# A four-layer hybrid encoder trunk on one core: first norm summed in x's own layout, output stored tile by tile, convolution state stored as rows

## The reference

```python
def rms_norm(x, gain):
    return x * rsqrt(mean(x * x, axis=-1) + 1e-6) * gain

for i in range(4):                                  # hp: prompt, hs: sample
    h = h + mixer_i(rms_norm(h, norm_mix[i]))
    h = h + square(relu(rms_norm(h, norm_mlp[i]) @ w_up[i])) @ w_down[i]
y = rms_norm(h, norm_final)

def short_conv_mix(h, conv_prefix, w_in, w_conv, w_out):
    gate_b, gate_c, xp = split(h @ w_in, 3)
    u_ext = concat([conv_prefix, gate_c * xp])
    y = w_conv[0] * u_ext[0:t] + w_conv[1] * u_ext[1:t+1] + w_conv[2] * u_ext[2:t+2]
    return (gate_b * y) @ w_out, u_ext[-2:]          # last 2 rows: the new state
```

## Time and profile before

| | |
|---|---|
| median of 3 runs | 2972.03 us (2965.87 to 2976.87) |
| profiled execution, its own time | 2968.8 us |
| its span | 2967.1 us |
| busy: TensorE, DVE, ScalarE, GpSimd | 96%, 43%, 29%, 9% |
| granted TensorE clock, mean | 0.982 |
| loaded, stored | 208.56 MB, 12.86 MB |
| slab of weights, issue to landing | 5.1 to 5.3 us, conv_w_out 15.4 (medians) |

### The profile page before, as it was taken

The page is one execution under the profiler, slowest core; times in us unless marked ns, Lnnn a source line. Parts: engine busy times, 40 slices in busy tenths (PEclk is TensorE's granted clock), DMA queues, the critical chain, the costliest instruction groups (busy, mean ns, idle before and its releaser), DMA issues.

```text
span 2967.1 us, 49404 instructions
## 1 busy us (share of the span) xinstructions
PE 2853.6 (96%) x21191; PEld 2767.3 (93%) x21191; DVE 1270.7 (43%) x1628; ACT 859.0 (29%) x891; POOL 258.5 (9%) x246
## 2 busy tenths in 40 slices
PE   5999999999999999999996789999999999999998
PEld 5987899999999999999996779999999878999997
DVE  3346443333455433334346554333443464433333
ACT  3126432222311322223123243212231264322222
POOL 5000100000112100001004430000010001000001
PEclk8999999999999999999998889999999999999999
DMA  3220232222223322222221012222232202322221
GB/s 122 82 74 1 72 112 77 85 85 85 84 73 71 85 86 85 77 80 85 74 70 50 1 60 83 85 85 86 72 99 85 75 1 72 117 73 84 85 85 46
DMA packets 205446, 223.39 MB, mean 75 GB/s; under 512 B 3734, under 2 KB 200416, under 8 KB 205312
## 3 DMA queue, kind: packets, MB, share of 16 engines
q1 hardware_dynamic: 200336, 203.70, 21.9%
q0 software_dynamic: 4976, 17.74, 1.8%
HBM read 208.56 MB, written 12.86 MB: 75 GB/s over the span
## 4 chain that ended last, share of the span: by engine, by line
PE 78%; issue 15%; DVE 3%; ACT 2%; POOL 1%; DMA 1%; POOLq 0%; DVEq 0%; SPq 0%; ACTq 0%
PE bank L347 67%; PE bank L453 4%; PE bank L427 2%; DMA raw<-in_conv_w_out 1%; PE bank L596 1%; POOL big L1443 1%; ACT big L802 1%; PE bank L484 1%; PE bank L420 1%; PE bank L641 0%; PE bank L650 0%; PE bank L638 0%; DVE stg L1246 0%; DVE stg L1273 0%; PE bank L547 0%
## 5 line engine op out<-in xcount | busy, mean ns | idle before, releaser
L347 PE MATMUL bank<-ahi,whi 128*128 128x288 f32 x3584 | 770.0, 296 | 7.0 <-DVE alo L1013 6.5
L347 PE MATMUL bank<-ahi,wlo 128*128 128x288 f32 x3584 | 767.2, 296 | 0.0
L347 PE MATMUL bank<-alo,whi 128*128 128x288 f32 x3584 | 766.9, 296 | 0.0
L689 ACT ACTIVATE whi<-raw 128x2048 fp32r<-128x2048 f32 x191 | 364.6, 1909 | 849.7 <-PE bank L347 838.4
L347 PEld LDWEIGHTS bank<-ahi,whi 128*128 128x128 f32 x3584 | 578.3, 189 | 9.9 <-DVE wlo L986 7.4
L347 PEld LDWEIGHTS bank<-alo,whi 128*128 128x128 f32 x3584 | 577.9, 189 | 0.0
L347 PEld LDWEIGHTS bank<-ahi,wlo 128*128 128x128 f32 x3584 | 577.7, 189 | 0.0
L347 PE MATMUL bank<-hhi,whi 128*128 128x288 f32 x2560 | 551.6, 297 | 15.6 <-DVE hlo L1163 9.5
L347 PE MATMUL bank<-hhi,wlo 128*128 128x288 f32 x2560 | 549.9, 296 | 0.0
L347 PE MATMUL bank<-hlo,whi 128*128 128x288 f32 x2560 | 549.9, 297 | 0.0
L986 DVE TENSOR_TENSOR wlo<-raw,whi 128x2048 fp32r<-128x2048 f32 x192 | 440.2, 2293 | 252.0 <-ACT whi L689 250.0
(11 more groups left out here) (252 smaller groups left out, 1769.5 us busy)
## 6 DMA issues: line engine op xcount, KB each, us to landing
raw<-in_mlp_w_up SPq DMA_DIRECT2D x64, 1024.0 KB, 5.3
raw<-in_mlp_w_down SPq DMA_DIRECT2D x64, 1024.0 KB, 5.1
raw<-in_sb_w_qkv SPq DMA_DIRECT2D x24, 1024.0 KB, 5.1
raw<-in_conv_w_in SPq DMA_DIRECT2D x12, 1024.0 KB, 5.1
raw<-in_gla_w_in SPq DMA_DIRECT2D x12, 1024.0 KB, 5.3
raw<-in_sb_w_o SPq DMA_DIRECT2D x8, 1024.0 KB, 5.2
out<-mixs POOLq DMA_DIRECT2D x3, 2048.0 KB, 7.9
out<-big POOLq DMA_DIRECT2D x2, 2048.0 KB, 8.3
```

Of the source, the lines that this page charges most:

```text
L347: mm = pe.matmul(acc[h][:, 0:HALF], w[:, u, k, m * P:(m + 1) * P], a[:, k, h * HALF:(h + 1) * HALF], start=(k == 0 and w is whi and a is a ...
L689: act.activation(whi[:, 1 - u], raw[:, 1 - u], ACT.Copy).then_inc(w_hi, 1)
```

## The change

- **First norm.** ScalarE squares each x tile as it was loaded (tokens on partitions) and sums along the row (`token_squares`, result `x_sq` [128 x 5]). GpSimd multiplies `ident` with each column of `x_sq` into `ssq` (`token_sums`), so that `sum_squares` sums over a diagonal matrix. The eight `squared` and `add_squares(0)` are gone.
- **Start of the queues.** GpSimd makes `ident` first, then issues the vector loads, then the other constants and the sums; `rank_raw` and `CK` are issued behind them. TensorE's first transposes wait for `ident_ready` alone. ScalarE splits slab 0 before it evacuates the vectors.
- **Convolution state.** `tails` is transposed on TensorE behind the first chunk of layer 1's output projection, copied to `tails_t` [32 x 128] by DVE, and stored in four DMAs of 8 rows of 512 bytes behind `add_squares(3)`.
- **Output.** Chunks 0 to 5 of `big` are transposed between chunks of the last projection (chunks 0 to 3 of all tiles, and 4 and 5 of the prompt's), chunks 0 to 3 evacuated unscaled; the rest follows after it. The last square isn't added by GpSimd but summed by TensorE apart. Five DMAs on SyncE store one token tile each.

```diff
@@ -317,6 +321,12 @@
...
+    for t in range(NT):
+        dst, n = (y_prompt[0, t * P:(t + 1) * P, :], P) if t < 4 else (y_sample[0], TS)
+        sp.wait_ge(y_v, t + 2)
+        sp.wait_ge(y_a, t + 1)
+        sp.dma_start(dst, VT[0:n, t, :]).then_inc(y_stored, 16)
+    sp.wait_ge(y_stored, 16 * NT)
@@ -360,6 +370,8 @@
...
         pe.wait_ge(ssq_add, 9 * (i + 1))
+        if i == 0:
+            pe.wait_ge(const_ready, CONSTS)
@@ -371,7 +383,7 @@
...
-    pe.wait_ge(const_ready, CONSTS)
+    pe.wait_ge(ident_ready, 1)
@@ -651,6 +663,36 @@
...
+    def y_chunk(t, c, bk):
+        w = P if t < 4 else TS
+        i = c % 4 * P
+        return pe.transpose(bk[0:w, i:i + P], big[:, c, t * P:t * P + w], ident[:])
+    def y_transposes(s, m):
+        if (s, m) == (2, 0):
+            pe.wait_ge(y_ev, 4)
+            for t in range(4):
+                for c in range(4):
+                    mm = y_chunk(t, c, bank[4 + t])
+                mm.then_inc(y_tp, 1)
+        elif (s, m) == (2, 1):
+            pe.wait_ge(y_raw, 1)
+            for c in range(4):
+                mm = y_chunk(4, c, bank[4])
+            mm.then_inc(y_tp, 1)
+        elif (s, m) == (3, 0):
+            pe.wait_ge(y_ev, 6)
+            pe.wait_ge(y_raw, 5)
+            for t in range(4):
+                for c in (4, 5):
+                    y_chunk(t, c, bank[4 + t])
+    def tails_out_(s, m):
+        if (s, m) == (0, 0):
+            pe.wait_ge(tails_ready, KC)
+            pe.transpose(bank[4][0:4 * KC, 0:P], tails[:].rearrange("p j i c -> p (j i c)"), ident[:]).then_inc(tails_tp, 1)
@@ -660,22 +702,32 @@
...
         project(base + IN_SLABS, hhi, hlo, mix_ready, 8 * layer, OUT_SLABS,
-                between=keys_out(layer // 3) if layer in (0, 3) else None)
+                between=keys_out(layer // 3) if layer in (0, 3) else tails_out_ if layer == 1 else None)
...
             project(b, ahi, alo, xg_ready, 16 * layer + 8, OUT_SLABS, norm=2 * layer + 1 if g == 0 else None)
-            project(b + OUT_SLABS, hhi, hlo, hid_ready, 8 * (GROUPS * layer + g), OUT_SLABS)
-    pe.wait_ge(acc_free, 2 * SLABS + 4)
-    pe.wait_ge(ssq_add, 9 * 9)
+            project(b + OUT_SLABS, hhi, hlo, hid_ready, 8 * (GROUPS * layer + g), OUT_SLABS,
+                    between=y_transposes if (layer, g) == (3, GROUPS - 1) else None)
+    pe.wait_ge(y_ev, 7)
     for t in range(NT):
-        w = P if t < 4 else TS
-        mm = pe.matmul(bank[0][0:w, t:t + 1], ssq[:, t * P:t * P + w], negones[:, 0:1], start=True, stop=True)
-    mm.then_inc(norm_sum, 1)
+        for c in (6,) if t < 4 else (4, 5, 6):
+            y_chunk(t, c, bank[4 + t] if t < 4 else bank[0])
+    def row_sums(src, start):
+        for t in range(NT):
+            w = P if t < 4 else TS
+            mm = pe.matmul(bank[1][0:w, t:t + 1], src[:, t * P:t * P + w], negones[:, 0:1],
+                           start=start and t == 0, stop=not start, skip_group_check=True)
+        return mm
+    pe.wait_ge(ssq_add, 9 * 8 + KC)
+    row_sums(ssq, True)
+    pe.wait_ge(sq_ready, 8 * 8 + KC)
+    row_sums(sq_x, False).then_inc(norm_sum, 1)
     pe.wait_ge(y_ev, 8)
-    pe.wait_ge(norm_v, 5 * 8 + 1)
-    to_token_major(TB_Y, big, 0)
+    for t in range(NT):
+        y_chunk(t, 7, bank[4 + t] if t < 4 else bank[0]).then_inc(y_tp, 1)
@@ -739,18 +791,26 @@
...
+    def token_squares(t):
+        n = P if t < 4 else TS
+        act.wait_ge(x_in[t], 16)
+        act.activation(stg[0:n, 0:D], flat(0, 9)[0:n, t * D:(t + 1) * D], ACT.Square,
+                       accum_out=x_sq[0:n, t:t + 1]).then_inc(x_squared, 1)
+        act.wait_ge(x_squared, t + 1)
+    act.sem_inc(sq_ready, 8)
+    for t in range(4):
+        token_squares(t)
...
         evacuate(c, X[:, c, 0:TP], bank[c][:, :])
+    token_squares(4)
+    act.wait_ge(slab_in[0], 16)
+    act.activation(whi[:, 0], raw[:, 0], ACT.Copy).then_inc(w_hi, 1)
...
     act.wait_ge(ev_a, 5)
-    act.wait_ge(slab_in[0], 16)
-    act.activation(whi[:, 0], raw[:, 0], ACT.Copy).then_inc(w_hi, 1)
...
         gained(0, j, V_MIX)
-    for j in range(KC):
-        act.wait_ge(ssq_add, j + 1)
-        squared(0, j)
@@ -922,6 +982,12 @@
...
+    def y_unscaled(s, m):
+        for t in range(4) if (s, m) == (2, 0) else (4,) if (s, m) == (2, 1) else ():
+            w = P if t < 4 else TS
+            act.wait_ge(y_tp, t + 1)
+            act.activation(VT[0:w, t, 0:512], bank[4 + t % 4][0:w, :], ACT.Copy).then_inc(y_raw, 1)
@@ -967,12 +1034,10 @@
...
     act.wait_ge(norm_v, 5 * 8 + 5)
-    for n in range((TB_Y + 1) % 2, 10, 2):
-        t, g = n // 2, n % 2
-        w = P if t < 4 else TS
-        act.wait_ge(tp_ready, TB_Y + n + 1)
-        act.activation(VT[0:w, t, g * 512:(g + 1) * 512], bank[(TB_Y + n) % 8][0:w, :], ACT.Copy,
-                       scale=rt[0:w, t:t + 1]).then_inc(ev_a, 1)
+    for t in range(NT):
+        w, bk = (P, bank[4 + t]) if t < 4 else (TS, bank[0])
+        act.wait_ge(y_tp, NT + t + 1)
+        act.activation(VT[0:w, t, 512:1024], bk[0:w, :], ACT.Copy, scale=rt[0:w, t:t + 1]).then_inc(y_a, 1)
@@ -1321,6 +1386,11 @@
...
+    def tails_rows(s, m):
+        if (s, m) == (0, 0):
+            dve.wait_ge(tails_tp, 1)
+            dve.tensor_copy(tails_t[:], bank[4][0:4 * KC, 0:P]).then_inc(tails_out, 1)
@@ -1374,26 +1444,36 @@
...
+    dve.memset(rt_m[:], 1.0).then_inc(y_v, 1)
     dve.wait_ge(norm_sum, 9)
-    dve.memset(rt_m[:], 1.0).then_inc(y_ev, 1)
-    dve.wait_ge(y_ev, 9)
-    dve.tensor_scalar(rt_m[:, 0:4], bank[0][:, 0:4], -1 / (TRI * D), EPS, ALU.mult, ALU.add)
-    dve.tensor_scalar(rt_m[0:TS, 4:5], bank[0][0:TS, 4:5], -1 / (TRI * D), EPS, ALU.mult,
+    dve.wait_ge(y_v, 1)
+    dve.tensor_scalar(rt_m[:, 0:4], bank[1][:, 0:4], -1 / (TRI * D), EPS, ALU.mult, ALU.add)
+    dve.tensor_scalar(rt_m[0:TS, 4:5], bank[1][0:TS, 4:5], -1 / (TRI * D), EPS, ALU.mult,
...
     dve.wait_ge(norm_v, 5 * 8 + 5)
-    for n in range((TB_Y + 0) % 2, 10, 2):
-        t, g = n // 2, n % 2
+    dve.wait_ge(y_raw, NT)
+    for t in range(NT):
         w = P if t < 4 else TS
-        dve.wait_ge(tp_ready, TB_Y + n + 1)
-        dve.tensor_scalar(VT[0:w, t, g * 512:(g + 1) * 512], bank[(TB_Y + n) % 8][0:w, :], rt[0:w, t:t + 1],
-                          None, ALU.mult).then_inc(ev_v, 1)
+        dve.tensor_scalar(VT[0:w, t, 0:512], VT[0:w, t, 0:512], rt[0:w, t:t + 1], None,
+                          ALU.mult).then_inc(y_v, 1)
...
+    steps = [0]
+    def made(ins):
+        ins.then_inc(pool_step, 1)
+        steps[0] += 1
+        pool.wait_ge(pool_step, steps[0])
+    made(pool.memset(ident[:], 0.0))
+    pool.affine_select(ident[:], ident[:], [[-1, P]], ALU.not_equal, 1.0, base=0,
+                       channel_multiplier=1).then_inc(ident_ready, 1)
@@ -1404,32 +1484,18 @@
...
         row += n
-    pool.dma_start(rank_raw[:], gla_w_in[0].rearrange("(k p) c -> p k c", p=P)[:, :, 3 * D:3 * D + 16])\
-        .then_inc(rank_in, 16)
-    pool.dma_start(CK, cache_sb_k[0, 0].rearrange("(j p) h d -> p j (h d)", p=P)).then_inc(ck_in, 16)
-    steps = [0]
-    def made(ins):
-        ins.then_inc(pool_step, 1)
-        steps[0] += 1
-        pool.wait_ge(pool_step, steps[0])
-    made(pool.memset(ident[:], 0.0))
-    pool.affine_select(ident[:], ident[:], [[-1, P]], ALU.not_equal, 1.0, base=0,
-                       channel_multiplier=1).then_inc(const_ready, 1)
...
     pool.tensor_copy(sums[:, 0, :], tri[:]).then_inc(const_ready, 1)
+    pool.wait_ge(const_ready, 1)
...
     pool.tensor_scalar(maskb[:], mask01[:], 1.0, -MASKED, ALU.subtract, ALU.mult).then_inc(const_ready, 1)
-    pool.wait_ge(const_ready, 5)
+    pool.wait_ge(ident_ready, 1)
@@ -1437,12 +1503,24 @@
...
         pool.memset(ssq, 0.0).then_inc(ssq_add, 1)
-        with pool.Fori(0, KC) as j:
+        with pool.Fori(0, KC if i < 8 else KC - 1) as j:
...
-    add_squares(0)
+    def token_sums():
+        made(pool.memset(ssq, 0.0))
+        for t in range(NT):
+            n = P if t < 4 else TS
+            pool.wait_ge(x_squared, t + 1)
+            pool.tensor_scalar(ssq[0:n, t * P:t * P + n], ident[0:n, 0:n], x_sq[0:n, t:t + 1], None,
+                               ALU.mult).then_inc(ssq_add, 1)
+        pool.sem_inc(ssq_add, 4)
+    token_sums()
+    pool.dma_start(rank_raw[:], gla_w_in[0].rearrange("(k p) c -> p k c", p=P)[:, :, 3 * D:3 * D + 16])                .then_inc(rank_in, 16)
+    pool.dma_start(CK, cache_sb_k[0, 0].rearrange("(j p) h d -> p j (h d)", p=P)).then_inc(ck_in, 16)
@@ -1485,17 +1563,21 @@
...
                 pool.wait_ge(y_ready, 3 * (c - 1))
+            if c >= 2:
+                pool.wait_ge(tails_ready, c - 1)
...
             pool.tensor_copy(tails[:, 0, :, c], u[:, 512:514])
-            made(pool.tensor_copy(tails[:, 1, :, c], u[:, 578:580]))
+            pool.tensor_copy(tails[:, 1, :, c], u[:, 578:580]).then_inc(tails_ready, 1)
+    def tails_stored():
+        pool.wait_ge(tails_out, 1)
...
             for j, dst in ((0, conv_p), (1, conv_s)):
```

(14 more changed lines are left out.)

11 lines of the change are left out of this document (8 added, 3 removed).

## The result

| | before | after |
|---|---|---|
| median, us | 2968.95 (4 runs, 2962.03 to 2976.87) | 2924.99 (4 runs, 2923.11 to 2927.15) |
| profiled execution, us (span) | 2968.8 (2967.1) | 2927.15 (2925.4) |
| mean granted clock | 0.982 | 0.986 |

The ratio is 0.9851, 95% interval 0.9823 to 0.9879: 44 us faster. 2938 was forecast and 2929 to 2949 given as the range, so the sign held and the size did not. The two spans differ by 41.7 us, and they are taken apart here stage by stage.

What follows compares the result with a forecast made beforehand. TensorE, busy 96% of the span, was taken as the bound. Start 20.0, middle 8.1 and end 5.1 sum to 33.2 us: 2968.8 profiled becomes 2935.6, with 3.2 to the median 2938.8; forecast 2938, range 2929 to 2949.

Steps and rivals of the forecast that it cites:

- The three places: Start, convolution output weights in the middle, and end, where TensorE stands or runs at low clock: 20.0, 8.1 and 5.1 us.
- rival (a): Start: slab 0 no earlier, or GpSimd's masks slow the first splits; gain 14.4 instead of 20.0 us, 2944; chance 0.09.
- (d): First norm: sum of squares comes late on GpSimd and TensorE still stands some 10 us; 2948; chance 0.03.
- (e): First projection: the clock stays at its lower level throughout, 153 us lost; 3092; chance 0.01.
- rival (c): Middle: the slab is late for a reason other than the stores, so 8 us stay; 2946; chance 0.03.
- the bound of 8.4: Middle: upper bound in us on the gain from replacing the element-wise convolution-state stores, forecast at net 8.1, lower bound 6.
- From issue to span's end it is 9.7 us: End: time for storing 2.36 MB, read from the kernel before and kept for five stores, as splitting costs nothing.
- Rival (b): End: the five stores don't overlap, 25 us instead of 9.7, so 15 more; 2953; chance 0.09 with its milder form.
- The estimate of 15.4 us: End: store time if the skill's fixed cost of about 2.0 us per DMA came one behind the other; 2944.
- The rule against one step: End: skill's rule that transposes don't count for the clock gate, risking 2 us on row sums; the forecast followed the trace.
- The step that failed: Whole kernel: TensorE's matmuls keep their time, so only its standing and low-clock time can be won; 33.2 us in all.
- at 6.40 us each: First projection: time per chunk of 48 matmuls, kept from before, 147.2 us for the 23 remaining chunks.

Runs made afterwards that it cites:

- old_sum: The changed kernel with the first norm sum made as before, by ScalarE squares and GpSimd additions; its first projection ends at 189.6 us, where the change's ends at 174.99.
- loads_early: The changed kernel with the loads of rank_raw and the key cache issued right behind the vector loads, as before; 2923.14 us, first matmul 3.3 us later.
- stores_late: The kernel before, its element-wise convolution-state stores issued where the change issues its row stores; 8.2 us gained, 7.4 of them lost again by the next layer.
- pool_stores: The changed kernel with its five output stores issued from GpSimd's queue instead of SyncE's; span 2922.8 us, ending 15.7 behind the last projection matmul.
- one_store: The changed kernel with the output stored by SyncE as two stores behind the last scaling, instead of five; span 2938.6 us, ending 15.7 behind the last projection matmul.
- the pair with the pace fixed: The change and the kernel before, each with three 48-column matmuls and one 192-column matmul added per projection following a norm sum; 2940.64 and 2979.74 us, both slow-paced.
- pace_probe2: The changed kernel with one unread matmul of 24, 40 or 48 columns behind the third chunk of each of the 32 MLP projections; span 2921.0 us.

## Why the prediction was right or wrong

- **Which places to read.** The three places were the right ones, and each gave what its rows said: 20.5, 8.1 and 6.7 us against 20.0, 8.1 and 5.1.
- **Start.** Slab 0 landed at 13.3 (13.5 forecast), the first matmul came at 18.51 (18.6), and the second chunk at 27.75 (28.2). old_sum splits this into 14.6 for the sum and 5.9 for the rest, and rival (a) is out. The rest is 3.3 for the loads, shown by loads_early, and, as the difference, about 2.6 for the order of the start, which wasn't tried alone. Rivals (d) and (e) did not happen.
- **Middle.** The slab landed in a median of 4.9 us, and no wait and no low clock followed. stores_late adds that the pieces and not the moment of the stores are the cause, so rival (c) is out. The size varies with the execution, from 8.1 to 12.9 us, as the jammed slab takes 32.8 to 36.8 to land; the bound of 8.4 was read from one execution and was too tight.
- **End.** 5.3 to the first store was forecast as 5.4, and 3.0 us for 28 transposes was met as well. The step that was mis-sized is "From issue to span's end it is 9.7 us": that row was a store by GpSimd, and by SyncE it is 8.2. pool_stores brings 9.9 back. Rival (b) is out: five stores took 8.2 us from the first issue to the end, and one_store's two took 8.1. The estimate of 15.4 us beside it put the stores one behind the other, which neither queue did: from GpSimd five took 9.9.
- **The rule against one step.** The row sums stand behind seven transposes, and the granted clock over them is 1.00. Twenty records take 2.20 us, where ten took 2.15 before. The chain's row and the stretch:

```profile
2912.69 2.20 PE bank L720 x20
```

```profile
2913.00:2915.00 2.00, 2.00 (x19) 1.94 (x19) 0.44 (x4) 0.56 (x1) 0.00 (x0) 1.00 0.00 0
```

 So the choice held. For the rule of the Trainium skill, "TensorE: Matmul & The Clock Gate", Part 4, it is a weak test, since here the transposes follow long matmuls closely.
- **The step that failed** is "its matmuls are untouched by this change, so what can be won is the time in which it stands or runs at the lower of its two clock levels". In the sum it is the constant of "at 6.40 us each": matmuls that the change does not touch were put at the same time as before, and a second pace at the same clock at nothing. For the first projection the constant held, 147.24 against 147.2. But untouched matmuls run at 130.0 or 133.3 ns, for up to 3072 in a row, and which of the two mostly changes by nanoseconds at the third chunk behind a norm sum. In the first two profiles this was worth 7.8 us net.
- **How the 13.8 us between the sum's 2938.8 and the measured 2924.99 add up, to 0.1.** 7.8 are the pace. 5.4 are the step from the profiled execution to the median: the prediction added 3.2, as before, and the change's median lay 2.2 below. 2.1 are the three parts, and the linear attention takes 1.4 back. Without the pace the result would have been 2932.8, inside the range; that it fell below is in part luck.
- **The range.** The spread of one kernel was taken as "4 of the runs". The change's 14 executions lie between 2913 and 2938. Its own gain, by the pair with the pace fixed, is 36 us by the stages and 39 by the medians, where 34 were forecast. From the 2975 at which the kernel before had its median over all 50 runs that is 2936 to 2939: the forecast was near the mark for the change and wrong about how well one median knows it.

What stays open: why the slow pattern has its 140 ns, and whether the change's code falls into the fast pace more often than the kernel before. Two of its three profiles have a fast MLP and the one of the kernel before has none, which are too few.

## What to carry to other kernels

When TensorE bounds a kernel, compare matmul counts of equal stretches at the same granted clock before you credit an edit with a gain: code that you did not touch may have changed pace, and a total is then worth no more than its stage sums. Stores in 4-byte pieces jammed the loads beside them at both places where they were issued, so transpose first and store rows, and keep loads that nobody waits for out of the first ten microseconds. A store that ends the kernel should leave from SyncE, as early as its first tile is ready.

## What the runs showed of the hardware

- Matmuls of 128x288 (fp32r), each with its own weight load, run back to back at 133.3 or at 130.0 ns at the same granted clock of 1.00. One matmul of 24 to 48 columns with 128 weight columns (27 ns) turns one into the other: fast to slow 13 of 13 times in pace_probe2, slow to fast 16 of 16 times with the 140 ns interval right ahead of it. 64 to 224 columns, 8 or 4 columns, or 64 and fewer weight columns, did not start the fast pace. The Trainium skill, "TensorE: Matmul & The Clock Gate", "Wait — 56ns, not 53.3ns?", gives columns / 2.4 GHz + 2.5 ns between the starts of matmuls at the full clock, which makes an estimate of 122.5 ns for 288 columns; both paces of this stream are above it.
- Four stores of 1024 elements each at 4 bytes apiece jammed the DMA engines enough to delay a 1 MB load to 32.8 to 36.8 us (median 5), and another to 29.0 us when issued later; as 8 rows of 512 bytes each, the same four stores left it at a median of 4.9.
- 2.36 MB of stores take 8.2 us from first issue to the end of the span by SyncE's queue and 9.9 by GpSimd's, from the same five issues.
- A Square that also sums its row costs 1.06 us for 1024 columns and 0.19 more for reading the sum out.
